# A hybrid attention and mLSTM kernel on one core: squares summed by ScalarE, one result buffer per block in the context attention, and four row slots in the first projection

## What is computed

```python
h = layer_norm(x) * (1 + scale) + shift                       # both streams
q, ga, k, v, u, gb = split(h @ w_in)                          # 768, 768, 256, 256, 256, 256 columns
q = rms_norm(q.reshape(b, t, 12, 64), q_gain)                 # a sum of squares for each head of 64 columns
k = rms_norm(k.reshape(b, t, 4, 64), k_gain)
ql, kl = apply_rope(ql, cos, sin), apply_rope(kl, cos, sin)   # image tokens
y_lat = merge(attention(ql, [kc, kl], [vc, vl]), gal, fourier_mix(rms_norm(ul)), gbl)
y_ctx = merge(attend(qc, kc, vc), gac, fourier_mix(rms_norm(uc)), gbc)   # 256 queries, 256 keys, 12 heads
# then the output projection and a residual norm, and a second layer with two mLSTM scans
```

## Time and profile before

| | us |
|---|---|
| median of 3 runs | 3933.68 (3932.98 to 3936.29) |
| the profiled execution, its time | 3935.59 |
| the profiled execution, its span | 3933.8 |
| projection of layer 0 | 36 to 591 |
| heads | 591 to 784 |
| attention of the context | 784 to 851 |
| PE busy, share of the span | 3566.1, 91% |
| DVE busy, share of the span | 2199.5, 56% |
| ACT busy, share of the span | 1257.8, 32% |

### The profile page before, as it was taken

One profiled execution on the slowest core, in us unless ns is written; L12 is line 12 of the kernel. 1 busy time (PEld: TensorE's weight loads), 2 busy tenths in 40 slices (PEclk: granted clock), 3 DMA queues, 4 the chain that ended last, 5 costly groups with the idle time before them and its releaser, 6 DMA issues. The chain is left out here.

```text
span 3933.8 us, 50682 instructions
## 1 busy us (share of the span) xinstructions
PE 3566.1 (91%) x17340; PEld 2691.9 (68%) x17340; DVE 2199.5 (56%) x3429; ACT 1257.8 (32%) x1782; POOL 1446.9 (37%) x913
## 2 busy tenths in 40 slices
PE   6999994579999999999949969999999995999698
PEld 4788772255666666666648857888998884887586
DVE  4533228946676667667636655333334443777576
ACT  2322322314444444444420024222223331564300
POOL 1100005507776776777633421000000001444355
PEclk8999995569999999999979989999999997999899
DMA  5221119811111111111045433221211112767564
GB/s 187 95 72 65 67 48 286 259 47 31 40 33 33 32 41 32 32 37 36 23 142 198 162 120 103 70 70 70 79 56 56 46 35 74 231 218 244 203 209 143
DMA packets 313500, 395.98 MB, mean 101 GB/s; under 512 B 81788, under 2 KB 210188, under 8 KB 313184
## 3 DMA queue, kind: packets, MB, share of 16 engines
q1 hardware_dynamic: 281760, 319.09, 25.9%
q10 hardware_dynamic: 21184, 37.46, 3.0%
q0 software_dynamic: 10368, 36.97, 2.3%
HBM read 269.76 MB, written 121.20 MB: 99 GB/s over the span
## 5 line engine op out<-in xcount | busy, mean ns | idle before, releaser
L235 PE MATMUL pj_acc<-pj_whi,pj_h_hi 128*128 128x512 f32 x1808 | 710.5, 393 | 5.7 <-DVE pj_h_lo L479 5.7
L1043 DVE TENSOR_REDUCE al_mx<-al_sx 128x1 f32<-128x512 f32 (+1 forms) x960 | 562.4, 632 | 267.8 <-PE al_sx L1120 254.4
L236 PE MATMUL pj_acc<-pj_wlo,pj_h_hi 128*128 128x512 f32 x1808 | 706.4, 391 | 0.0
L237 PE MATMUL pj_acc<-pj_whi,pj_h_lo 128*128 128x512 f32 x1808 | 706.2, 391 | 0.0
L988 ACT ACTIVATE al_e<-al_st 128x1024 f32<-128x1024 f32 x432 | 443.1, 1026 | 578.0 <-PE al_st L1133 568.7
L479 DVE TENSOR_TENSOR pj_h_lo<-pj_hall,pj_h_hi 128x1024 fp32r<-128x1024 f32 x258 | 375.1, 1455 | 288.3 <-ACT pj_h_hi L374 288.3
L433 POOL TENSOR_TENSOR pj_wlo<-pj_wst,pj_whi 128x2048 fp32r<-128x2048 f32 x28 | 128.7, 4595 | 959.9 <-ACT pj_whi L358 959.9
L1018 POOL TENSOR_TENSOR al_acc_p<-al_acc_p,al_e 128x1024 f32<-128x1024 f32 x192 | 457.0, 2380 | 20.0 <-POOL al_acc_p L1014 0.4
L374 ACT ACTIVATE pj_h_hi<-pj_hall 128x1024 fp32r<-128x1024 f32 x258 | 270.9, 1055 | 537.1 <-PE pj_acc L237 519.7
L1142 PE MATMUL al_acc<-al_e,vres 128*64 128x512 f32 x1728 | 402.5, 601 | 0.0
L235 PEld LDWEIGHTS pj_acc<-pj_whi,pj_h_hi 128*128 128x128 f32 x1808 | 341.9, 189 | 77.6 <-DVE pj_h_lo L479 6.5
(11 more groups left out here) (282 smaller groups left out, 5671.9 us busy)
## 6 DMA issues: line engine op xcount, KB each, us to landing
s_proj<-pj_stage SPq DMA_DIRECT2D x162, 256.0 KB, 2.0
pj_wst<-in_w ACTq DMA_DIRECT2D x28, 1024.0 KB, 5.6
ml_k<-s_proj SPq DMA_DIRECT2D x36, 512.0 KB, 4.3
ml_v<-s_proj SPq DMA_DIRECT2D x36, 512.0 KB, 8.8
mo_in<-s_proj SPq DMA_DIRECT2D x34, 512.0 KB, 6.3
hm_w<-in_ada_w SPq DMA_DIRECT2D x16, 1024.0 KB, 8.0
ml_qt<-s_qt SPq DMA_DIRECT2D x32, 512.0 KB, 6.1
s_h<-ml_h POOLq DMA_DIRECT2D x32, 512.0 KB, 8.0
```

Source lines behind the costliest of these rows:

```text
L235: nc.tensor.matmul(out, s_hi, m_hi, start=start, stop=False)
L236: nc.tensor.matmul(out, s_hi, m_lo, start=False, stop=False)
L237: return nc.tensor.matmul(out, s_lo, m_hi, start=False, stop=stop)
L1043: V.tensor_reduce(mx[:, x:x + 1], slots[x % NSX][:, 0:spans[x % NS][1]], AX.X, ALU.max).then_inc(sx_max, 1)
```

## The change

Three parts, all in layer 0.

1. *Projection.* RING is 4 in both layers, and the preparation goes two steps ahead in layer 0 too, outside chunk 0.
2. *Heads.* ACT squares each group of 64 columns in an operation of its own, 20 for a tile instead of 2, and each gives the group's sum with it (`accum_out`), written to `ss`. DVE's `sums` and the semaphore `ss_done` are gone; POOL's norms wait for `sq_done`. Squares wait for `rs_done` of two tiles before, since they now write `ss`.
3. *Attention of the context.* `o` has a buffer for each of the 12 blocks and DVE doesn't wait for stores; the 24 row DMAs are issued by POOL, block by block as `negm` comes, and no more by SP.

```diff
-    K, RING, NST, NACC, PIECES, NX = len(steps), 2 if L0 else 4, 3, 3, 2, 3
+    K, RING, NST, NACC, PIECES, NX = len(steps), 4, 3, 3, 2, 3
...
-    ahead = [min(K - 1, k + (1 if L0 or c == 0 else 2)) for k, (c, _) in enumerate(steps)]
+    ahead = [min(K - 1, k + (1 if c == 0 else 2)) for k, (c, _) in enumerate(steps)]
...
             def squares(n):
                 act.wait_ge(ld[n % NR_RAW], 32 * (n // NR_RAW) + 32)
+                if n >= 2:
+                    act.wait_ge(rs_done, n - 1)
+                r = raw[:, n % NR_RAW, :]
                 if n:
-                    act.wait_ge(ss_done, n)
-                r = raw[:, n % NR_RAW, :]
-                nc.scalar.activation(sq[:, 0:NHD], r[:, 0:C_V].rearrange("p (h d) -> p h d", d=HD), ACT.Square)
-                nc.scalar.activation(sq[:, NHD:], r[:, C_U:C_GATE].rearrange("p (h d) -> p h d", d=HD), ACT.Square).then_inc(sq_done, 1)
+                    act.wait_ge(sq_done, n)
+                for i in range(NS):
+                    at = i * HD if i < NHD else C_U + (i - NHD) * HD
+                    x = nc.scalar.activation(sq[:, i, :], r[:, at:at + HD], ACT.Square, accum_out=ss[:, n % 2, i:i + 1])
+                x.then_inc(sq_done, 1)
...
-                pool.wait_ge(ss_done, n + 1)
+                pool.wait_ge(sq_done, n + 1)
...
-            def sums(n):
-                dve.wait_ge(sq_done, n + 1)
-                if n >= 2:
-                    dve.wait_ge(rs_done, n - 1)
-                V.tensor_reduce(ss[:, n % 2], sq[:], AX.X, ALU.add).then_inc(ss_done, 1)
...
-    o = m.sb(tag + "o", [P, 2, nq, HD])
+    NO = 2 if LAT else TOTAL
+    o = m.sb(tag + "o", [P, NO, nq, HD])
...
-            row(0, 0)
-            if not LAT:
-                for n in range(1, TOTAL):
-                    row(n, n)
+            if LAT:
+                row(0, 0)
...
+            else:
+                pool.wait_ge(zero_done, 1)
+                for n in range(TOTAL):
+                    pool.wait_ge(negm_done, n + 1)
+                    for i in range(nq):
+                        pool.dma_start(qb[HD:HD + 1, n, i * P:(i + 1) * P].bitcast(F32), negm[:, n, i:i + 1].bitcast(F32)).then_inc(row_ld[n], 16)
...
-                if not (fixed(n) and n < 2):
+                if LAT and not (fixed(n) and n < 2):
                     dve.wait_ge(stored[p % 2], v * 16)
-                V.tensor_tensor(o[:, p % 2], fo[:, 0:nq * (HD + 1)].rearrange("p (s d) -> p s d", s=nq)[:, :, 0:HD],
+                V.tensor_tensor(o[:, p % NO], fo[:, 0:nq * (HD + 1)].rearrange("p (s d) -> p s d", s=nq)[:, :, 0:HD],
```

More of the change, by code:

```diff
@@ L616, in heads @@
     fixed_done, g_done, gf_done, table_done = (m.sem("hd_" + x) for x in ("fixed", "g", "gf", "table_done"))
-    sq_done, ss_done, eps_done, rs_done = (m.sem("hd_" + x) for x in ("sq_done", "ss_done", "eps_done", "rs_done"))
+    sq_done, eps_done, rs_done = (m.sem("hd_" + x) for x in ("sq_done", "eps_done", "rs_done"))
     px_done, turn_done, rot_done, un_done = (m.sem("hd_" + x) for x in ("px_done", "turn_done", "rot_done", "un_done"))
@@ L806, in _ @@
             V.tensor_scalar(g4[:, 2:4], g4[:, 2:4], float(HD) ** 0.5, None, ALU.mult).then_inc(g_done, 1)
-            sums(0)
             products(0)
@@ L816, in _ @@
                     turned(n)
-                if n + 1 < NT:
-                    sums(n + 1)
                 if n:
@@ L940, in store @@
                 rows = bass.ds((q0 + (n % nb) * nq) * P, W)
-                sp.dma_start(s["attn"][rows, bass.ds(h * HD, HD)].rearrange("(t p) d -> p t d", p=P), o[:, p % 2]).then_inc(stored[p % 2], 16)
+                sp.dma_start(s["attn"][rows, bass.ds(h * HD, HD)].rearrange("(t p) d -> p t d", p=P), o[:, p % NO]).then_inc(stored[p % 2], 16)
             for n in range(QB):
@@ L1027, in body @@
             def body(g, n, p, v, nxt):
-                if LAT:
-                    sums(n, p)
+                sums(n, p)
             if LAT:
                 over_blocks(pool, body)
+            else:
[4 more added lines that the diff above has]
+                        pool.dma_start(qb[HD:HD + 1, n, i * P:(i + 1) * P].bitcast(F32), negm[:, n, i:i + 1].bitcast(F32)).then_inc(row_ld[n], 16)
         @block.vector
```

## The result

| | before | changed |
|---|---|---|
| median | 3933.85 us (3932.98 to 3936.29) | 3896.64 us (3890.36 to 3897.25) |
| the profiled execution | 3935.59 | 3897.25 |
| its span | 3933.8 | 3895.6 |

The ratio of the changed kernel to the one before is 0.9897, interval 0.9885 to 0.991: 37 us, 1% faster.

A forecast was written before the change was run, and what follows sets the result against it. PE, busy 91%, was taken to bound the kernel, except where it waits or DVE sets heads' pace. Projection -7.7, heads -11.5 and context attention -17.6 sum to -36.8: 3898.8, less 1.9 for the median, 3896.9 us; range 3888 to 3919.

The forecast's parts named there:

- projection: Layer 0's projection: two 3.0 us PE stalls and the slow clock behind them (1.6 and some 0.1 us) go, -7.7.
- heads up to the DMA-bound turn: Heads until 661 us: six tiles save 1.40 each, less 1.8 at the start and two late turns of 2.2: -2.2.
- the DMA-bound turn: Heads' stretch at 661 us, where DVE waits for earlier stores; it ends when the DMAs have drained, so no gain.
- heads after it: Heads behind the DMA-bound stretch: nine tiles x 1.40 less one late turn of 2.2, less 1.1 for DMAs.
- context attention, first to last block start: Context attention: no wait for a store, -5.3, and five more starts 2.14 instead of 3.91 us apart, -8.9.
- its tail: End of the context attention, 837.59 to 847.54: PE's some 7.5 us shrink by 0.45 at the faster clock, -3.4.
- The late turns: Heads turns 3, 5 and 15: squares stand behind ACT's wait for PE's row product, 2.2 us late each.
- the 1.1 us taken off for the DMAs: Heads after the DMA-bound stretch: tiles ask for 361 GB/s, which fits barely, so 1.1 us of gain was deducted.
- stay hidden: Context attention: POOL's row DMAs, 24 at 0.62 us, cost nothing up to some 1.35 us each.
- the clock stays low in the context attention: Rival: blocks 2 to 11 stay 3.91 us apart, that part gives nothing, time 3915.6 us; chance 0.28.
- ACT as the pace of heads: Rival: a short squaring costs 0.30 to 0.40 us, heads gives from -4 to +18, time 3904 to 3926; chance 0.12.
- DMAs that bind heads throughout: Rival: heads' tiles stay near 8.8 us, heads gives -4, time 3904.4 us; chance 0.06.

The follow-up runs named there:

- e_proj: The kernel before with the projection part alone (four row slots, two steps ahead); 3929.26 us, ratio 0.9987.
- e_ring: The kernel before with four row slots in layer 0's projection but still one step ahead; 3937.44 us, ratio 1.0007.
- b_spread: The changed kernel with the key-row and v loads moved from turn 4 of heads to turns 13 to 16; 3887.32 us, ratio to before 0.9885.
- e_gap2: The changed kernel with a DVE pause of about 4.9 us before block 4's result in the context attention; 3912.76 us, one execution.
- e_ac: The kernel before with both context attention edits (twelve result buffers, row DMAs on POOL); 3921.26 us, ratio 0.9958.
- e_rows: The kernel before with the context attention's row DMAs on POOL, still two result buffers; 3919.87 us, ratio 0.9953.
- e_heads: The kernel before with the short squarings of heads alone; 3922.33 us, ratio 0.9968.
- e_buf: The kernel before with twelve result buffers in the context attention, row DMAs still on SP; 3918.21 us, ratio 0.9944.
- e_act10: The changed kernel with ten more short squarings per tile of heads; 3912.44 us, ratio 0.9937 to before.

## Why the prediction was right, point by point

Predicted 3896.9 us, measured 3896.64. The sum was -36.8; the profiled executions lie 38.3 apart. That the two times agree within 0.3 us is luck: heads gave 3.8 us more and the context attention 1.9 less than forecast, the start of the projection, which no term covered, took 1.4 back and varies by 7 us between profiles, and none of the changed kernel's four executions took the 15 us or more of the low clock. What was forecast and came out is each stage's mechanism. The terms:

| term | predicted | measured |
|---|---|---|
| projection | -7.7 | -8.5 with the changed kernel, -7.7 in e_proj |
| heads up to the DMA-bound turn | -2.2 | -4.8 |
| the DMA-bound turn | 0 | 0.0 |
| heads after it | -9.3 | -10.5 |
| context attention, first to last block start | -14.2 | -14.3 |
| its tail | -3.4 | -3.1 |
| its beginning | 0 | +1.7 |
| start of the projection (no term) | | +1.4 |

Of the forty slices of the page before, one more is as low in PE as those of heads (4 tenths, 1967 to 2065 us); no part of the change touches it.

**Projection.** The mechanism and its size were right. The means of all profiles are 536.7 without the part (six) and 529.0 with it (eight), 7.7 us. e_ring adds that the second step does it and not the slots. The 0.1 us for a slow clock behind the second stall stands on no row: there the clock reads 1.00 from 466.5 us on.

**Heads, ACT.** A short squaring was taken at 0.24, rounded up to 0.25, from an overlap seen on other shapes; it is 0.24. This was the choice on which most hung (0.14 to 0.44), and it came out since the readout, 0.19 us, is nearly as long as the smallest ACT operation of the earlier trace rows, 0.20, and overlaps like the squarings of the earlier trace rows. No row ahead of the result showed this form, so the choice was a well-founded guess.

**Heads, sizes.** 3.8 us more came than predicted, from three terms. The start was to be 1.8 us later and is 0.3 later (first squaring to first `scaled` 9.00 instead of 8.69 us): the working left out POOL's two norm instructions, which are shorter now, 0.28 and 3.55 us instead of 1.67 and 3.87. In the kernel before the first of them started beside DVE's product (L760) and ended 0.09 us behind it. It isn't every DVE operation that does this: started beside DVE's low parts (L800) the same two take 0.23 and 3.55. The late turns were to cost 2.2 each and cost 1.68, 1.32 and 1.32: the chain was 16.9 us long (9.8 to ACT's store of the row, then 1.0, 4.8 and 1.3) instead of 17.3, and DVE wants its end after 2 x 7.75 instead of 15.4 or less. And the 1.1 us taken off for the DMAs weren't needed: 390 GB/s went through. That the long turn gave nothing, as forecast, is in part luck: where its code is the same it takes from 18.9 to 23.3 us in the profiles. That it is bound by DMAs was right, but the earlier trace rows show only DVE waiting for ACT; the stores and loads are in SP's rows above, and b_spread, without the loads there, has no long turn.

The Trainium skill's 358 GB/s (DMA: Bandwidth & Descriptors, Specifications), half of what the stack gives its two cores, would make such a tile 7.8 us, an estimate. The tile took 7.75 us at 369 to 390 GB/s, with one core running, so the trace doesn't bear that figure out as a limit here.

**Context attention.** The prediction held that the clock falls for the pause and for nothing else; e_gap2 shows the first, and the eight profiles in which it rose and no pause followed the second. Where it failed is the sentence that POOL's row DMAs "stay hidden": they do as far as their own landing goes, but beside them SP's loads of q land later, and the first block starts 17.8 us after the memset instead of 16.1 (18.1 in e_ac and 18.2 in e_rows, 16.2 in e_proj, 16.1 in e_heads, 16.2 in e_buf). It also gave the whole gain to the buffers and none to the rows on POOL; either would have done.

**Rivals.** That the clock stays low in the context attention is real: it had 0.28, and happened in 4 of 14 profiles, though in one only of the ten with an edit of this stage. Its price was well put: +18.7 then, and 17.4 by the stage's lengths (64.6 against 47.2). That it didn't happen in the changed kernel's executions was partly luck. ACT as the pace of heads begins at 0.32 us a squaring, where 0.24 was measured; at 0.36 the gain in heads is gone (e_act10), near the prediction's "at 0.33 it gives nothing". DMAs that bind heads throughout: not seen, DVE is busy for 7.72 of 7.75 us.

## What to carry to other kernels

- Before you free an engine from a wait, look at what the wait does to the clock behind it: a pause of 5 us cost 15 here, and the clock's fall was most of it.
- A shift of work to an engine with time to spare is best priced as a period, work of a tile against the pace of a tile, plus the turns in which that engine waits for something else; here 6.2 against 7.75 us, and three turns that a reordering then removed.
- Of two edits for one wait, test each alone: the second (row DMAs on POOL, beside the twelve buffers) brought nothing and cost 1.3 us.

## What the runs showed of the hardware that I had not expected

- A readout of the accumulator, 0.19 us, hides under its neighbours but for 0.09 us: a squaring of 64 columns with its sum costs 0.24 us from start to start (0.15 to its readout, 0.09 to the next squaring).
- TensorE can be busy without a break for 38 us and be granted 0.50 all along (e_proj, 793 to 831 us); the same instructions ran at 1.00 in other profiles.
- Little traffic from a second issuing engine can delay loads: beside POOL's 24 row DMAs of 512 bytes SP's loads of 128 KB took 3.1 to 3.7 us to land (medians of seven profiles) instead of 2.3 or 2.4, and the first block started 17.8 to 18.9 us after the memset instead of 16.1 to 16.4.
- POOL's add of 128x20 took 0.23 us beside DVE's low part and 1.67 when it started beside DVE's product (L760), which it outlasted by 0.09 us (before, 600.17 us).
- The beginning of the program, up to the first matmul of the projection, varies by 7 us between the profiles (57.2 to 64.6), as much as the projection part is worth; the lengths of projection and heads in kernels with the same code for them agree within 4 us, mostly within 1. What lies behind the last `o` varies by 4.4 us.
